# Sliding-window sample attention: a position's keys and values in one 4 KB row, two sequences on chip, keys transposed in two parts

## The reference, cut to what matters

```python
SWA_GROUPS = ((128, 1), (512, 4), (2048, 16))        # window, dilation
# cache_swa_w{W}: (1, 8, W, 2, 4, 128) float32: position, key or value, head, element
kv_g = concatenate([cache[g], kv_new], axis=1)
kv = take(kv_g, key_pos)                             # every dil-th position of the window, and itself
s = einsum('bqhd,bqjhd->bhqj', q, kv[:, :, :, 0]) * SWA_SCALE + bias
e = exp(s - max(s)); den = sum(e)
o = einsum('bhqj,bqjhd->bqhd', e / den, kv[:, :, :, 1])
```

## Time and profile before

| | us |
|---|---|
| median of 3 runs | 3238.17 (3235.86 to 3247.95) |
| the profiled execution | 3221.25 |
| its span | 3219.5 |
| the block `swa_sample` in it | 602 to 817 |

### The profile page before, as it was taken

The page is one execution under the profiler, slowest core; times in us unless marked ns, Lnnn a source line. Parts: engine busy times, 40 slices in busy tenths (PEclk is TensorE's granted clock), DMA queues, the critical chain, the costliest instruction groups (busy, mean ns, idle before and its releaser), DMA issues. The chain is left out here.

```text
span 3219.5 us, 44082 instructions
## 1 busy us (share of the span) xinstructions
PE 2829.5 (88%) x17313; PEld 2319.3 (72%) x17313; DVE 1509.3 (47%) x3597; ACT 544.4 (17%) x1380; POOL 614.8 (19%) x647
## 2 busy tenths in 40 slices
PE   5977699777797699999899997978869999989997
PEld 3544435555355499999899994636469999989997
DVE  1311100322203289889755532041249979965553
ACT  2333200444014121121000001012211111100000
POOL 0000130000000013334433310000003324443330
PEclk8788899899899899999999998989989999999998
DMA  4467896799848329989899975145535989989995
GB/s 126 153 202 246 266 323 240 201 279 246 298 160 298 131 95 382 365 317 351 297 409 409 409 300 183 53 170 200 182 132 218 377 320 345 352 329 409 409 409 194
DMA packets 276790, 867.86 MB, mean 270 GB/s; under 512 B 33014, under 2 KB 56599, under 8 KB 274044
## 3 DMA queue, kind: packets, MB, share of 16 engines
q1 hardware_dynamic: 197368, 589.89, 52.1%
q0 software_dynamic: 79216, 275.16, 22.7%
HBM read 846.23 MB, written 109.08 MB: 297 GB/s over the span
## 5 line engine op out<-in xcount | busy, mean ns | idle before, releaser
L2309 PE MATMUL ps<-xT,p1e_uT 128*128 128x192 f32 x2048 | 345.6, 328 | 9.4 <-DMA p1e_uT<-in_peer_uT 8.7
L2309 PE MATMUL ps<-xT,p0e_uT 128*128 128x192 f32 x2048 | 345.0, 328 | 9.6 <-DMA p0e_uT<-in_peer_uT 8.9
L2309 PEld LDWEIGHTS ps<-xT,p0e_uT 128*128 128x128 f32 x2048 | 333.6, 191 | 12.5 <-DMA p0e_uT<-in_peer_uT 10.8
L2309 PEld LDWEIGHTS ps<-xT,p1e_uT 128*128 128x128 f32 x2048 | 334.0, 191 | 11.8 <-DMA p1e_uT<-in_peer_uT 10.5
L2335 PE MATMUL ps<-p0e_S,p_qT 128*128 128x192 f32 x2048 | 337.1, 327 | 5.8 <-DMA p_qT<-in_peer_v 5.8
L2335 PE MATMUL ps<-p1e_S,p_qT 128*128 128x192 f32 x2048 | 337.2, 327 | 5.7 <-DMA p_qT<-in_peer_v 5.7
L2335 PEld LDWEIGHTS ps<-p1e_S,p_qT 128*128 128x128 f32 x2048 | 332.9, 190 | 9.9 <-DMA p_qT<-in_peer_v 9.8
L2335 PEld LDWEIGHTS ps<-p0e_S,p_qT 128*128 128x128 f32 x2048 | 332.4, 190 | 10.3 <-DMA p_qT<-in_peer_v 10.3
L2113 DVE SCALAR_TENSOR_TENSOR h_tok<-p0e_rows,p0e_dots,h_tok 128x1024 f32<-128x1024 f32 x127 | 163.1, 1284 | 142.8 <-DMA p0e_rows<-in_peer_v,p0e_expert 142.0
L2113 DVE SCALAR_TENSOR_TENSOR h_tok<-p1e_rows,p1e_dots,h_tok 128x1024 f32<-128x1024 f32 x127 | 163.1, 1284 | 141.4 <-DMA p1e_rows<-in_peer_v,p1e_expert 140.6
L2003 POOL DMA_INDIRECT p0e_rows<-in_peer_u,p0e_expert x128 | 153.1, 1196 | 382.5 <-DVE p0e_dots L2102 205.0
(11 more groups left out here) (458 smaller groups left out, 3619.4 us busy)
## 6 DMA issues: line engine op xcount, KB each, us to landing
p_qT<-in_peer_v SPq DMA_DIRECT2D x256, 512.0 KB, 7.3
p0e_uT<-in_peer_uT SPq DMA_DIRECT2D x128, 512.0 KB, 6.7
p1e_uT<-in_peer_uT SPq DMA_DIRECT2D x128, 512.0 KB, 6.7
out_swa_sample<-in_cache_swa_w SPq DMA_DIRECT2D x32, 2040.0 KB, 18.1
m_cache<-in_cache_mem_kv SPq DMA_DIRECT2D x32, 1024.0 KB, 12.0
ms_pages<-in_cache_mla SPq DMA_DIRECT2D x128, 144.0 KB, 2.5
ss_kcache<-in_cache_swa_w SPq DMA_DIRECT2D x72, 256.0 KB, 12.1
ss_vcache<-in_cache_swa_w SPq DMA_DIRECT2D x72, 256.0 KB
```

Source lines behind the costliest of these rows:

```text
L2309: mm = pe.matmul(k.ps[:, SB[i % len(SB)], 0:TD], ur[:, i % NU, c, :], k.xT[:, c, D0:T], start=(c == 0), stop=(c == KC - 1))
```

## The change

Keys and values of a position are loaded together as one row of 4 KB, 13 loads of 512 KB a sequence. There are two such buffers, for even and odd sequences. To make room, the queries and keys of the samples (`sample_qk`) are copied by GpSimd into the free `xT` during the block before (2 copies), `swa_qT` and `kT` are released, and four tiles of the odd buffer lie in `h_tok` and `xT`. The loads of sequence `u+1` wait for `values(u-1)` as a whole. On TensorE only seven groups of keys of `u+1` are transposed before `values(u)`; the other six and `score(u+1)` come behind it.

```diff
@@ attend_sample, sync
+            if a["shared"]:
+                load_values(0)
             load_keys(0)
             for u in range(DEC_B):
+                if a["shared"] and u + 1 < DEC_B:
+                    load_values(u + 1)
                 if u + 1 < DEC_B:
                     load_keys(u + 1)
-                load_values(u)
+                if not a["shared"]:
+                    load_values(u)
@@ attend_sample, tensor
                 if u + 1 < DEC_B:
-                    turn_keys(u + 1)
+                    turn_keys(u + 1, 0, FIRST_TURNED)
                 if u > 0:
                     turn_out(u - 1)
-                if u + 1 < DEC_B:
+                if u + 1 < DEC_B and FIRST_TURNED == G:
                     score(u + 1)
                 values(u)
+                if u + 1 < DEC_B and FIRST_TURNED < G:
+                    turn_keys(u + 1, FIRST_TURNED, G)
+                    score(u + 1)
@@ attend_sample, scalar
-                    take_keys(u + 1, 1 - slot)
+                    take_keys(u + 1, 1 - slot, 0, FIRST_TURNED)
...
                 if u + 1 < DEC_B:
+                    take_keys(u + 1, 1 - slot, FIRST_TURNED, G)
                     exponential(u + 1)
@@ attend_sample, vector
-                if u + 1 < DEC_B:
+                if u + 1 < DEC_B and FIRST_TURNED == G:
                     maxima(u + 1, (u + 1) % 2)
                 dve.wait_ge(o_ready, u + 1)
                 wait(dve, o_turned, u)
                 dve.tensor_copy(o_tok[:, :], k.ps[:, 6, 0:a["out_cols"]]).then_inc(o_taken, 1)
+                if u + 1 < DEC_B and FIRST_TURNED < G:
+                    maxima(u + 1, (u + 1) % 2)
@@ Stores.gpsimd
-        pass
+        for dst, src in self.keep:
+            pool.tensor_copy(dst, src)
@@ swa_sample
+        N, KEY_PARTS = len(SWA_TILES), [3, 2, 4, 4]
+        own = k.sb(ctx, "ss_cache", [P, 2 * N - 4, 2 * GW])
...
+            srcs = [c[0]] + [c[1][i * P:(i + 1) * P] for i in range(4)] + [wide[i, :, 0:8, :] for i in range(8)]
+            j0 = sum(KEY_PARTS[:part])
+            for j in range(j0, j0 + KEY_PARTS[part]):
+                sp.dma_start(tiles[slot][j], srcs[j]).then_inc(landed, 16)
...
-            "key_parts": [5, 4, 4], "key_dmas": [2, 4, 4], "load_keys": load_keys, "shared": False, "slots": 1,
-            "load_values": load_values, "value_dmas": 11, "stage": stage, "n_stage": 2,
+            "key_parts": KEY_PARTS, "key_dmas": KEY_PARTS, "load_keys": load_keys, "shared": True, "slots": 2,
+            "first_turned": 7, "load_values": load_values, "value_dmas": 1, "stage": stage, "n_stage": 2,
```

More of the change, by code:

```diff
@@ L786, in attend_sample @@
         parts = a["key_parts"]
+        FIRST_TURNED = a.get("first_turned", len(a["groups"]))
         NL, AHEAD = a.get("ring", 2), a.get("n_ahead", 0)
@@ L854, in _, with turn_keys @@
         def _(pe):
-            def turn_keys(u):
+            def turn_keys(u, g0=0, g1=G):
                 slot, lane = u % 2, u % NL
                 starts = [sum(parts[:j]) for j in range(len(parts))]
-                for g, blocks in enumerate(a["groups"]):
+                for g, blocks in list(enumerate(a["groups"]))[g0:g1]:
                     if g in starts:
@@ L932, in _, with take_keys @@
         def _(act):
-            def take_keys(u, slot):
-                for g in range(G):
+            def take_keys(u, slot, g0=0, g1=G):
+                for g in range(g0, g1):
                     act.wait_ge(turned, G * u + g + 1)
@@ L1345, with __init__ @@
 class Stores:
-    def __init__(self, begin, sem, due, ahead=None):
-        self.begin, self.sem, self.due, self.ahead = begin, sem, due, ahead
+    def __init__(self, begin, sem, due, ahead=None, keep=()):
+        self.begin, self.sem, self.due, self.ahead, self.keep = begin, sem, due, ahead, keep
     def sync(self, sp):
@@ L1586, in mla_sample, with swa_sample @@
         })
-def swa_sample(k, e, swa_qT, kT):
+def swa_sample(k, e, sample_qk, free):
     nc, io = k.nc, k.io
     with ExitStack() as ctx:
-        kcache = k.sb(ctx, "ss_kcache", [P, len(SWA_TILES), GW])
-        vcache = k.sb(ctx, "ss_vcache", [P, len(SWA_TILES), GW])
-        vnew = k.sb(ctx, "ss_vnew", [DEC_S, 3 * GW])
+        N, KEY_PARTS = len(SWA_TILES), [3, 2, 4, 4]
+        own = k.sb(ctx, "ss_cache", [P, 2 * N - 4, 2 * GW])
+        vnew = k.sb(ctx, "ss_vnew", [DEC_S, 2, 3 * GW])
+        spare = [k.h[:, i, :] for i in range(3)] + [free]
+        tiles = [[own[:, j, :] for j in range(N)], [own[:, j, :] for j in range(N, 2 * N - 4)] + spare]
         KT = k.sb(ctx, "ss_kT", [P, SWA_H, SWA_CACHED])
@@ L1601, in setup_pool, with load_keys @@
             pool.wait_ge(done, 1)
[L1603 to L1604 removed]
+        def load_keys(sp, u, slot, part, landed, _):
+            c = [io[n][0, u].rearrange("w c h d -> w (c h d)") for n in
                  ("cache_swa_w128", "cache_swa_w512", "cache_swa_w2048")]
[L1606 to L1609, removed]
             wide = c[2].rearrange("(i a r) n -> i a r n", i=8, r=16)
[L1612 to L1616, removed]
+            srcs = [c[0]] + [c[1][i * P:(i + 1) * P] for i in range(4)] + [wide[i, :, 0:8, :] for i in range(8)]
+            j0 = sum(KEY_PARTS[:part])
+            for j in range(j0, j0 + KEY_PARTS[part]):
+                sp.dma_start(tiles[slot][j], srcs[j]).then_inc(landed, 16)
         def load_values(sp, u, slot, landed):
[L1619 to L1621 removed]
+            sp.dma_start(vnew[:, slot, :], io["kv_new"][u * DEC_S:(u + 1) * DEC_S, 3 * GW:6 * GW]).then_inc(landed, 16)
         def stage(pool, u, slot, staged):
[L1624 to L1626 removed]
+            t = slice(DEC_S * u, DEC_S * (u + 1))
+            pool.tensor_copy(qst[:, slot, :, 0:DEC_S], sample_qk[:, 0, :, t]).then_inc(staged, 1)
+            pool.tensor_copy(knew[:, slot, :, :], sample_qk[:, 1, :, t]).then_inc(staged, 1)
         def q(g, h):
@@ L1649, in values @@
         def values(j, h):
-            return lambda slot: vcache[:, j, h * P:(h + 1) * P]
+            return lambda slot: tiles[slot][j][:, GW + h * P:GW + (h + 1) * P]
         value_terms = [(PAD * h, PAD, SWA_D, j, P, PAD * h, values(j, h))
@@ L1661, in swa_sample @@
             "bias": lambda c0, n: e["bias_s"][:, c0:c0 + n],
-            "groups": [[(lambda slot, j=j, h=h: kcache[:, j, h * P:(h + 1) * P], P) for h in range(SWA_H)]
+            "groups": [[(lambda slot, j=j, h=h: tiles[slot][j][:, h * P:(h + 1) * P], P) for h in range(SWA_H)]
                        for j in range(len(SWA_TILES))],
```

14 lines of the change are left out of this document (9 added, 5 removed).

## The result

The changed kernel takes 3338.12 us (median of four runs, 3332.07 to 3341.76), the kernel before 3242.49 on the same chip: a ratio of 1.0289 with a 95% interval of 1.0252 to 1.0327. That is 96 us slower; 3245 was forecast, and the range ended at 3266.

A forecast was written before the change was run, and what follows sets the result against it. Loads set the pace before, just ahead of TensorE; afterwards a TensorE chain would. 632.2 start + 7 x 25.0 rounds + 15.7 end = 822.9 against 816.7, +6.2 us, so 3245 us; range 3228 to 3266.

The forecast's parts named there:

- Only the block of the window attention over the sample caches changes.: Whole kernel: only this block, 602 to 823 us, would change; everything outside was held to be untouched.
- a change outside 602 to 823: Sign of being wrong: any change in time outside the window block's 602 to 823 us, held to be untouched.
- The bounds are 275 … and 409 …: Wide-tile loads at 4 KB: between 275 and 409 GB/s, so 15.2 to 10.3 us for the eight tiles.
- I take 325: Wide-tile loads at 4 KB: 325 GB/s assumed, 12.9 us for the eight tiles of a sequence.
- a want at 15.8: Window block round: TensorE wants part three's tiles 15.8 us after release; they were to land at 16.0.
- The wide rival: Window block: wide tiles stay at about 275 GB/s, part three lands late, rounds 26.3 us; +18 us, 3256; chance 0.20.
- The chain, 24.2 to 25.4 us a round: TensorE in the window block: scores, softmax and values in sequence set each round, 24.2 to 25.4 us, taken as 25.0.
- the 3.70 us wait on ScalarE: Window block: TensorE waits about 3.7 us each round for ScalarE's key copies, which stand behind the exponential.
- First scores at 30.0 us after the block's first load: Window block's start: sequence 0's scores end at 632.2, between 629.7 and 634.7 by the two wide rates.
- End 15.7: Window block after the last score: 5.6 softmax, 3.3 transposes, 5.8 values, 1.0 copies, together 15.7 us.
- The low clock of the rival: TensorE, window block: clock stays low through each round's values, round 27.7 us; +26 us, 3264; chance 0.11.
- No speed of loading can take more than 24.2 - 20.6 = 3.6 us from a round in this order of work: Kernel before, window block: rounds 24.2 us, TensorE's own work 20.6, so faster loads gain at most 3.6 a round.

The follow-up runs named there:

- the run with fast 4 KB loads: The changed kernel with page numbers read ahead of the wait and each wide tile read from 128 successive (wrong) positions, against the kernel before: 3240.78 us, ratio 1.001.

## Why the prediction was wrong, point by point

- **"Only the block of the window attention over the sample caches changes."** This step failed and is the larger part, 1.7 to 1.8%. The diff edited a loop that another block runs through the same flag. The order of that block's queue was shown by none of my rows, since I compared the two kernels only where I expected the change. The price is mechanical: 9.6 us of register reads, moved from before a wait to behind it, every round. The last of the prediction's own signs of being wrong, a change outside 602 to 823, is what came.
- **"The bounds are 275 … and 409 …", "I take 325".** This step failed too: 239 was measured, below the lower bound, and it is the other 1.05%. I took the 64 KB jumps of the source for the cause of 275, and a larger piece for a cure. The cause is the form of the load, which the change kept. (That it is the form and not the gaps was shown with 2 KB pieces.) Part three, the sixth to the ninth tile (the prediction calls it the eighth and ninth, but counts its 2.10 MB), landed 21.2 us after release (719.5 to 740.67) where I had 16.0, against a want at 15.8. The lower bound was the rate of another piece size in that form, and so no bound.
- **The wide rival** (26.3 us a round, chance 0.20) had the mechanism and the place right; its size was off: rounds of 29.5 us ((907.52 - 701.23)/7, between ends of scores). At 239 part three would land 18.3 us after release (3.0 + 6.5 + 8.8), not the measured 21.2. Most of the rest is a straggler: all but two of the part's 64 landings are in by 738.45, the next comes at 739.37 and the last, for which TensorE waits, at 740.62. The estimate from the Trainium skill, "DMA: Bandwidth & Descriptors", section "Why small descriptors are slow (HBM only)", was 281 and spoke against the change; the trace went further, to 239. What the Trainium skill says in "Perfetto Trace Analysis", section "DMA Optimizations", that larger transfers gain, was not borne out in this form: 276 became 239.
- **The chain, 24.2 to 25.4 us a round.** Right, as the run with fast 4 KB loads shows (24.3 to 25.4), with the 3.70 us wait on ScalarE in its place. So the change would have been level at best: it gave up an order with 20.3 us a round.
- **First scores at 30.0 us after the block's first load.** Measured 36.3 (701.23 - 664.9), for the same reason: with fast wide tiles it was 28.5. **End 15.7:** 17.3 (924.8 - 907.52). Sum: 36.3 + 206.3 + 17.3 = 259.9.
- **Clock.** The low clock of the rival came, but in the waits and the transposes around them: 0.50 from 731 to 744. The value products behind them kept full clock (1.00 from 745 on; 72 of them in 2.17 us at 746.45, where the cold ones of the last sequence took 4.02). The rival's mechanism did not happen.
- **"No speed of loading can take more than 24.2 - 20.6 = 3.6 us from a round in this order of work".** Right but for 0.3 us, and it was the gain to be had: from the first to the seventh sequence, where the 24.2 was read, rounds fell to 20.3.

What stays open: why a load of 16 blocks by 8 rows is slow. The Trainium skill, "DMA: Bandwidth & Descriptors", section "The descriptor swizzle", says that a transfer to 128 partitions gives each engine partitions of one SBUF port only. Were a load of 16 by 8 dealt by blocks, each engine would write eight neighbouring partitions, and pairs of engines would share two ports. This fits the runs, but no trace shows which engine writes which partition, so it is argued, not shown. No run tells either whether reading or writing is the slow side, nor why 4 KB pieces suffer more than 2 KB ones in this form. In the traces 48 and 60 KB between blocks gave rounds of 28 us where 36 and 128 KB gave 24 to 25; these are single executions, and the traced one at 60 KB took 3249.25 us against a median of 3229.07, so no effect of the distance can be read from them.

## What to carry to other kernels

A line changed in a shared loop is changed for all that run it: before you cost the part that the change is about, compare the order of instructions over the whole program, above all what used to stand ahead of a wait. Where loads are slower than others of the same size, try the form of the load before the size of its pieces: cut the data so that the source is 128 rows at one constant step, one to a partition. A rate measured in one form and piece size is no bound for another.

## What the runs showed of the hardware that I had not expected

- 2 KB pieces with 64 KB between them run at 391 GB/s in loads of one row of 128, and at 274 to 276 in loads of 16 blocks by 8 rows; where such blocks overlap and leave no gap, at 248.
- In the latter form 4 KB pieces move 239 GB/s, less than 2 KB ones at 274 to 276.
- Loads with a slowest dimension of 8 from SyncE's queue had eight landings each besides the one near their issue, and in stretches ran at half the DMA share (0.52 to 0.53) and 195 to 206 GB/s. From GpSimd's queue the share was 1.03 and the rate 217 (651 to 790).
- Sixteen reads of page numbers by SyncE took 9.6 us, 0.6 us each, by the gap that they left between two loads (219.85 to 229.44) and that closed to 0.55 us when they were moved.
